# Unused columns between the on-chip tensors of a two-layer block: new start addresses for the split activations and the large region

## The reference, cut to what matters

```python
def reference(x, ...):
    x = first_block(x, ...)      # SSD (Mamba-2) branch + short-conv branch, then a gated FFN
    return second_block(x, ...)  # compressed/selected/window attention + latent attention, then a gated FFN

# what fills the time are linear layers on h, 256 positions wide:
proj = h @ w_in                                       # 1024 x 10272
y_ssd, y_sc = y @ w_ssd_out, s @ w_sc_out
mix = (g_ssd * y_ssd + g_sc * y_sc) @ w_o
u = causal_dwconv(h @ w_up, ffn_conv_w, ffn_conv_b)   # 1024 x 5632
f = (silu(u_gate) * u_val) @ w_down                   # 2816 x 1024
```

## The kernel before, in words

| tensor | begins at | length |
|---|---|---|
| ring | 16512 | 16384 |
| WH, WHF | 32896 | 16384 |
| WL, WLF | 49280 | 16384 |
| adaring | 65664 | 16384 |
| par | 82048 | 15140 |
| X | 97216 | 8192 |
| SQ | 105408 | 8192 |
| HR, HX | 113600 | 16384 |
| RR, R | 129984 | 90112 |
| CT | 220096 | 4096 |
| eps_col | 227680 | 4 |
| mlars | 227712 | 128 |
| kct | 228000 | 120 |
| identb | 228128 | 256 |

## Time and profile before

### The profile page before, as it was taken

One profiled execution on the slowest core, in us unless ns is written; L12 is line 12 of the kernel. 1 busy time (PEld: TensorE's weight loads), 2 busy tenths in 40 slices (PEclk: granted clock), 3 DMA queues, 4 the chain that ended last, 5 costly groups with the idle time before them and its releaser, 6 DMA issues.

```text
span 1111.3 us, 22886 instructions
## 1 busy us (share of the span) xinstructions
PE 1051.7 (95%) x8357; PEld 993.7 (89%) x8357; DVE 562.8 (51%) x1165; ACT 642.6 (58%) x1140; POOL 692.6 (62%) x306
## 2 busy tenths in 40 slices
PE   3999999999899989999999999998998889999998
PEld 2999999988789979999998999896665689999998
DVE  5877425589774454555423432495263724444400
ACT  3555754477764576666546557735576546666532
POOL 0787888812268847888786487660220065888795
PEclk9999999999999999999999999999899999999999
DMA  9988677656427855676677387567211033555463
GB/s 372 380 283 287 245 292 285 224 184 209 168 99 268 263 204 171 228 242 223 217 258 252 110 286 278 174 206 293 98 40 38 1 117 129 195 186 188 162 208 106
DMA packets 63650, 226.84 MB, mean 204 GB/s; under 512 B 6976, under 2 KB 8160, under 8 KB 63328
## 3 DMA queue, kind: packets, MB, share of 16 engines
q1 hardware_dynamic: 62384, 221.74, 57.1%
q10 hardware_dynamic: 1200, 4.23, 1.3%
HBM read 224.86 MB, written 1.08 MB: 203 GB/s over the span
## 4 chain that ended last, share of the span: by engine, by line
PE 67%; issue 16%; POOL 8%; ACT 3%; DMA 2%; DVE 2%; SPq 1%; POOLq 0%; ACTq 0%; DVEq 0%
PE psL L550 64%; POOL WL L503 8%; DMA R<-ada_w 1%; PE psS L550 1%; PE psO L550 1%; DMA ring<-wts 1%; SPq L405 1%; ACT WH L1042 1%; ACT R L1153 0%; ACT L1033 0%; ACT HR L1074 0%; SPq L390 0%; POOL R L530 0%; PE psS L839 0%; DVE HR L1649 0%
## 5 line engine op out<-in xcount | busy, mean ns | idle before, releaser
L503 POOL TENSOR_TENSOR WL<-ring,WH 128x1024 fp32r<-128x1024 f32 (+1 forms) x282 | 672.2, 2398 | 306.4 <-ACT WH L1042 245.5
L550 PE MATMUL psL<-HR,WH 128*128 128x256 f32 x3056 | 545.4, 281 | 5.7 <-POOL WL L503 2.5
L550 PEld LDWEIGHTS psL<-HR,WH 128*128 128x128 f32 x3056 | 468.2, 188 | 10.3 <-POOL WL L503 4.4
L550 PE MATMUL psL<-HR,WL 128*128 128x256 f32 x1528 | 428.1, 280 | 0.0
L550 PEld LDWEIGHTS psL<-HR,WL 128*128 128x128 f32 x1528 | 288.3, 189 | 0.0
L1042 ACT ACTIVATE WH<-ring 128x1024 fp32r<-128x1024 f32 (+1 forms) x210 | 216.1, 1040 | 100.9 <-PE psL L550 84.5
L550 PE MATMUL psL<-RR,WH 128*128 128x256 f32 x1344 | 240.8, 282 | 6.1 <-POOL WL L503 4.5
L550 PEld LDWEIGHTS psL<-RR,WH 128*128 128x128 f32 x1344 | 206.9, 189 | 7.7 <-issue 3.9
L550 PE MATMUL psL<-RR,WL 128*128 128x256 f32 x672 | 188.8, 281 | 0.0
L1328 ACT ACTIVATE WH<-ring 128x1024 fp32r<-128x1024 f32 (+1 forms) x88 | 92.9, 1055 | 86.8 <-PE psL L550 86.8
L1909 DVE SCALAR_TENSOR_TENSOR CT<-psL,par,CT 128x254 f32<-128x254 f32 (+1 forms) x176 | 81.0, 480 | 116.7 <-ACT CT L1331 111.3
(11 more groups left out here) (255 smaller groups left out, 1103.5 us busy)
## 6 DMA issues: line engine op xcount, KB each, us to landing
ring<-wts SPq DMA_DIRECT2D x289, 512.0 KB, 3.7
adaring<-ada_w SPq DMA_DIRECT2D x80, 512.0 KB, 4.8
R<-ada_w SPq DMA_DIRECT2D x16, 512.0 KB, 12.6
ring<-wts SPq DMA_DIRECT2D x16, 384.0 KB, 3.4
R<-cum_dram ACTq DMA_DIRECT2D x8, 512.0 KB, 4.3
ring<-wts SPq DMA_DIRECT2D x8, 288.0 KB, 3.7
adaring<-wts SPq DMA_DIRECT2D x1, 2048.0 KB, 9.4
WHF<-wts SPq DMA_DIRECT2D x2, 1024.0 KB, 7.8
```

Of the source, the lines that this page charges most:

```text
L503: nc.gpsimd.tensor_tensor(WL[:, k, 0:n], ring[:, k, 0:n], WH[:, k, 0:n].bitcast(F32), SUB).then_inc(lo_done, 1)
L550: return nc.tensor.matmul(out, lhsT, rhs, start=start, stop=stop)
```

## The change

`PAR_SPEC` gets a last entry of 7 columns that nothing reads, with zeros as its contents. A tensor of 13 fp32 columns (52 bytes) that nothing uses is allocated ahead of HR and HX, and one of 9 columns (36 bytes) ahead of RR and R. Every instruction stays as it is but for the addresses, and the second parameter load is 7 columns wider.

```diff
--- before.py
+++ after.py
@@ -157,7 +157,7 @@
     ("q_gain", 128), ("ks_gain", 128), ("kw_gain", 128), ("kc_gain", 128), ("mq_gain", QK), ("mk_gain", QK),
     ("causal_add", P), ("causal01", P),
     ("cos", 2 * 128), ("sin", 2 * 128), ("mcos", 2 * 64), ("msin", 2 * 64),
-    ("cmask_add", 2 * NCMP), ("cmask01", 2 * NCMP), ("sel", 2 * NCMP),
+    ("cmask_add", 2 * NCMP), ("cmask01", 2 * NCMP), ("sel", 2 * NCMP), ("pad", 7),
 ]
 PAR = {}
 _n = 0
@@ -193,10 +193,12 @@
         par = sb("par", [P, NPAR])
         X = sb("X", [P, KD, T])
         SQ = sb("SQ", [P, 2048])
+        sb("lead_in_h", [P, 13])
 
         with nc.sbuf_tensor("HR", [P, 4096], F32R) as HR:
             pass
         HX = sb("HX", [P, 4096])
+        sb("lead_in_r", [P, 9])
         with nc.sbuf_tensor("RR", [P, 22528], F32R) as RR:
             pass
         R = sb("R", [P, 22528])
@@ -2350,6 +2352,7 @@
         "cos": cos, "sin": sin, "mcos": mcos, "msin": msin,
         "cmask_add": f(np.where(seen, 0.0, -1e30)), "cmask01": f(seen),
         "sel": np.tile(np.eye(32, 2 * NCMP, dtype=np.float32), (4, 1)),
+        "pad": np.zeros((P, 7), np.float32),
     }
     assert all(v[n].shape == (P, c) for n, c in PAR_SPEC), [(n, v[n].shape) for n, c in PAR_SPEC if v[n].shape != (P, c)]
     return np.ascontiguousarray(np.concatenate([v[n] for n, _ in PAR_SPEC], axis=1))
```

## The result

| | before | after |
|---|---|---|
| median of 11 runs each, us | 1105.53 | 1118.56 |
| lowest, highest | 1098.87, 1116.22 | 1110.61, 1125.03 |
| ratio after / before | | 1.0108, 95% interval 1.0070 to 1.0146 |
| the profiled execution's own time | 1113.12 | 1110.61 |
| its span, mean granted clock | 1111.3, 0.986 | 1108.7, 0.991 |

The account below looks back on a forecast made before the run. PE, busy 95% of the span, was taken as the bound, its time matmul count times step. Terms of 0 us on PE and 0.04 us hidden left the median at 1105.5 us, range 1098 to 1114.

Parts of the forecast that it names:

- the placing rule: Every tensor begins at a multiple of 32 bytes, so HR moves by 64 bytes, RR by 128, both staying multiples of 64.
- the instruction order: In every engine's order, no instruction is added, removed or moved; three allocations differ in length or are new.
- POOL: POOL's L503 touches only ring, WH and WL, which don't move: cost 0.
- the parameter load and its cover: Second parameter load: 28 bytes more per partition, +0.04 us, hidden by 2.0 us before its first reader, ACT's L1093.
- DVE's and ACT's times: Engines writing HR and HL, writing and reading RR: a shift that keeps multiples of 64 costs 0.
- PE, 6600 matmuls with the moving operand shifted, 432 with the stationary one: 6600 x 0 = 0: PE's matmuls reading HR or RR: no change of step, 0 us, with far bounds of -29.7 and +29.7 us.
- Both reasons given for the 0: PE's step stays even at 117.7 and 117.8 ns across block starts in two tensors, and across the 88-column matmuls' starts.
- The 88-column matmuls: Last token chunk: moving blocks 352 bytes apart, starts 0, 32, 64, 96 beyond multiples of 128, yet 112.0 ns each.
- B: Rival, slower: weight load and moving read beginning alike disturb each other on HR's 4584 matmuls, up to +20.6 us; chance 0.06.
- A: Rival, faster: the 4.5 ns are an address effect and the new place is good; 1075.8 us for both tensors; chance 0.09.
- the question open at all: Token stage, HR stationary and weights moving: 113.2 ns a matmul against 117.7, same shape and clock, 4.5 ns unexplained.
- the base: Starting time for the forecast: median of the three runs shown, 1105.53 us, 7.6 us under the profiled execution's 1113.12.

Follow-up runs that it names:

- the map: Separate kernel, nothing else running: 96 matmuls of 128x256 for each of 45 start addresses of the moving operand; 113.4 ns at start 64, 120.0 at 128.

## Why the prediction was wrong

It gave 1105.5 us, no change, and a range to 1114. The measured 1118.56 lies above it.

- **Right:** the placing rule. The named offsets of 52 and 24 do not come about; HR moves by 64 bytes and RR by 128, and all is a multiple of 64 as before. The offsets made real cost 2.6%, not 0.4%.
- **Right:** the instruction order, POOL, the parameter load and its cover, DVE's and ACT's times.
- **Wrong, the step that failed:** "PE, 6600 matmuls with the moving operand shifted, 432 with the stationary one: 6600 x 0 = 0". It took "multiples of 64 as before" for "unchanged". Measured are +0.9 ns on 4584 matmuls (+4.1 us), +5.3 on 432 (+2.3) and, in the first profile, -4.4 on 55 units of RR (-5.9), with some 3.5 us of stretches at 113.3 that the kernel before has in some executions: +4.0 us or 1.004, against 1.0039 and 1.0042 measured. What changed was the distance between the starts of the two operands modulo 256, from 64 to 128 for HR. Both reasons given for the 0 were weak in the same way. The blocks within a tensor start 512 and 1024 bytes apart, and HR and RR both began 192 beyond a multiple of 256, so their even step says nothing about shifts of 64. The 88-column matmuls do vary the start by 32 bytes, but a third of the columns at 112.0 ns shows that the length of the moving stream does not set their step, and they kept 111 to 112 ns in the changed kernel, where the 256-column ones beside them went from 113.3 to 118.7. So they don't bear on the 256-column shape.
- **Of the token stage's 5.3 ns** the cause is shown less well than of HR's 0.9: all kernels with HR at 0 show it, but two kernels in which neither operand's start changed modulo 256 lost 4.4 ns there.
- **The rival that came true:** B in sign and place, at 0.06. Its mechanism, weight load and moving read that get in each other's way by how they begin, fits the steps by distance, but no run looks inside. Its price, up to 4.5 ns, was mis-sized: 0.9 ns on HR; and it left out the token stage's 5.3 ns. A came true beside it for RR (113.3 in down1, o2 and down2), and took most of B's loss back. The row named as making "the question open at all" was the right one: the 113.2 there and the 117.8 elsewhere are two of the steps in the map. A difference of 4% between two places with equal shapes and clock, with no wait to explain it, deserved more than 0.15 for A and B together.
- **Wrong, the base:** the median of three runs, 1105.53, against medians of 1111 to 1114 for the same kernel over 80 later runs. The text noted that one execution stood 7.6 us higher and took it for spread; it was nearer to the usual time. 1112 x 1.004 is 1116.4. Of the miss of 13 us some 6.5 are this, 4 to 5 the step above, and some 2 stay open.
- Not tested: what tips a stretch from 117.8 to 113.3 with the same starts, and the mechanism on the chip.

## What to carry to other kernels

Where PE-bound stretches of equal matmuls show a step above the smallest that the same trace has for that shape, try the operands' start addresses: place the moving operand at each multiple of 16 bytes within 256 in a small kernel with the real weights' start, read the step off the start times, and then place the tensor; here that gave 1.25% for one line. A start is not good or bad by itself: here it was good at 192 bytes ahead of the weights, modulo 256, and the same start with other weights was not. Check in the built program where a tensor lands before reasoning on its offset, since an allocator may round it. Compare medians only with the granted clocks beside them. And compare counts of matmuls in equal windows at the full clock, not spans, where executions differ by more than the effect.

## What the runs showed that was not expected

- One program takes different steps (113.3 or 117.8 ns) for the same stretch in different executions, evenly for 40 units, at full clock; 4.3 us hang on such a stretch alone.
- The step of a 128x256 matmul in this order takes values from 113.3 to 123.4 ns by the start of the moving operand, in a repeating pattern of 256 bytes that distinguishes single fp32 elements (0: 118.7, 4: 122.5, 12: 117.8).
- The weights' start counts as well. With both starts at multiples of 32 the distance between them, modulo 256, orders the steps (0: 120.0, 64: 117.8, 128: 118.7, 192: 113.3); at odd multiples of 16 it does not.
- With 32 weight columns in place of 128 the steps are up to 5 ns shorter, still uneven, and never under 113.3.
